# The S5 chain of a two-mixer block, moved ahead of the RWKV inverse

## What is computed

```
h = modulate(rms_norm(x), sh_m, sc_m);  proj = h @ w_in      # 1024 x 2304
z = proj[:, :1792];  u = proj[:, 1792:]                      # z: 14 tiles of 128, u: 4 tiles
z = z + mu * (shift(z) - z)
y_rwkv = group_norm(scan(S = S*w + (S a) b + v k)) + bonus, times a gate
s[t] = abar * s[t-1] + bbar u[t]       # S5: 32 groups of 16 channels, 64 complex states each
y = Re(c s) + d u;  zz = gelu(y);  out = zz * sigmoid(zz @ w_glu + b_glu)
y_s5 = rms_norm(out) * gain
x = x + g_m * (concat(y_rwkv, y_s5) @ w_out)
```

## Time and profile before

| what | us |
|---|---|
| median of 3 executions (1690.25 to 1692.58) | 1690.34 |
| profiled execution, its own time | 1687.02 |
| its span | 1685.2 |
| TensorE busy | 1507.8 |
| VectorE busy | 812.8 |
| ScalarE busy | 581.0 |
| GpSimd busy | 267.4 |

### The profile page before, as it was taken

The page is one execution under the profiler, slowest core; times in us unless marked ns, Lnnn a source line. Parts: engine busy times, 40 slices in busy tenths (PEclk is TensorE's granted clock), DMA queues, the critical chain, the costliest instruction groups (busy, mean ns, idle before and its releaser), DMA issues.

```text
span 1685.2 us, 23778 instructions
## 1 busy us (share of the span) xinstructions
PE 1507.8 (89%) x10024; PEld 1173.4 (70%) x10024; DVE 812.8 (48%) x1291; ACT 581.0 (34%) x1002; POOL 267.4 (16%) x224
## 2 busy tenths in 40 slices
PE   6979877877889999999989899998898999998989
PEld 3657666865668888888866687766686667766767
DVE  7783439623653233223354554546534455445552
ACT  4355231125333222222223434224522444232441
POOL 0000323000101011100012223222201233222220
PEclk9999987988999999999979999998998999999999
DMA  9212572162122222233221121111122111111121
GB/s 367 69 59 61 94 140 104 52 226 88 63 75 88 100 94 94 95 125 100 89 88 40 48 76 63 62 39 50 52 99 96 36 63 59 67 65 36 50 88 63
DMA packets 51849, 144.17 MB, mean 86 GB/s; under 512 B 13216, under 2 KB 17952, under 8 KB 50976
## 3 DMA queue, kind: packets, MB, share of 16 engines
q1 hardware_dynamic: 51744, 142.65, 26.4%
HBM read 137.95 MB, written 4.69 MB: 85 GB/s over the span
## 4 chain that ended last, share of the span: by engine, by line
PE 69%; DVE 14%; ACT 9%; issue 4%; POOL 2%; DMA 1%; SPq 0%; DVEq 0%; ACTq 0%
PE b L391 68%; ACT arena L2103 5%; DVE arena L1245 4%; DVE ring L1245 2%; DVE arena L1253 2%; ACT ring L2106 1%; PE b L394 1%; ACT L2103 1%; POOL arena L2734 1%; DVE arena L1933 1%; DVE X L1245 1%; ACT arena L2106 1%; DVE arena L2066 1%; DMA arena<-scr_yd 1%; DVE arena L1891 1%
## 5 line engine op out<-in xcount | busy, mean ns | idle before, releaser
L391 PE MATMUL b<-tile,ring 128*128 128x512 f32 x2288 | 702.9, 402 | 19.8 <-DVE ring L1245 9.2
L391 PE MATMUL b<-HR,ring 128*128 128x512 f32 (+1 forms) x1888 | 626.2, 408 | 63.1 <-DVE ring L1245 35.1
L391 PEld LDWEIGHTS b<-tile,ring 128*128 128x128 f32 x2288 | 437.5, 192 | 127.6 <-issue 19.5
L391 PEld LDWEIGHTS b<-HR,ring 128*128 128x128 f32 (+1 forms) x1888 | 363.6, 193 | 165.2 <-issue 61.0
L1245 DVE TENSOR_TENSOR ring<-ring,ring 128x1024 fp32r<-128x1024 f32 x186 | 256.1, 1379 | 299.9 <-ACT ring L2106 299.0
L391 PE MATMUL b<-arena 64*64 64x64 f32 (+10 forms) x3072 | 237.5, 289 | 42.9 <-issue 24.6
L2106 ACT ACTIVATE ring<-ring 128x1024 fp32r<-128x1024 f32 x186 | 195.7, 1054 | 213.9 <-PE b L391 213.4
L391 PEld LDWEIGHTS b<-arena 64*64 64x64 f32 (+5 forms) x3072 | 153.6, 150 | 115.8 <-issue 80.7
L2106 ACT ACTIVATE arena<-b 128x512 f32<-128x512 f32 (+3 forms) x136 | 74.4, 570 | 254.3 <-PE b L391 206.3
L1245 DVE TENSOR_TENSOR arena<-arena 128x512 f32<-128x512 f32 (+7 forms) x194 | 100.3, 549 | 71.2 <-ACT arena L2103 50.2
L2731 POOL TENSOR_TENSOR tile<-arena,tile 128x512 fp32r<-128x512 f32 x38 | 51.0, 1348 | 462.2 <-ACT tile L2106 462.2
(11 more groups left out here) (112 smaller groups left out, 1018.8 us busy)
## 6 DMA issues: line engine op xcount, KB each, us to landing
ring<-in_ws SPq DMA_DIRECT2D x218, 512.0 KB, 3.5
arena<-in_ws SPq DMA_DIRECT2D x15, 512.0 KB, 15.4
arena<-in_lw SPq DMA_DIRECT2D x2, 1280.0 KB, 5.6
X<-in_xT SPq DMA_DIRECT2D x2, 1024.0 KB, 6.2
arena<-scr_kpad SPq DMA_DIRECT2D x8, 256.0 KB, 12.5
X<-in_xT SPq DMA_DIRECT2D x1, 2048.0 KB, 15.3
outT<-X SPq DMA_DIRECT2D x8, 256.0 KB, 2.0
arena<-in_cst SPq DMA_DIRECT2D x1, 1088.0 KB, 5.0
```

What stands on the lines that cost most here:

```text
L391: return self.e.matmul(out, lhsT, rhs, start=start, stop=stop, skip_group_check=True)
```

## The change

The strings and the order of the tiles:

```diff
-PREP = "zpzpzpzpzp" + "zmzmpzmpzmpzpzpz"
-MIX = ("s" + "rrr" + "s" + "rrrr" + "a" + "rrrrrr" + "a" + "rs" * 4 + "rrs" * 5 + "a" + "rrs" * 4 + "a" + "rrs" * 6
-       + "rrrrr" + "a" + "rrrrs" + "rrrsr" + "a" + "r" + "s" + "rr" + "a" + "rr" + "s" + "rr" + "a" + "rr" + "a" + "ssss" + "ga"
-       + "s" + "g" + "s" + "oo" + "g" + "oo")
+U_TILES = [14, 15, 16, 17]
+PREP = "zpzzpz" + "smzpm" + "szpmzp" + "ssss" + "zps" + "zpss" + "zpss" + "zps" + "zps"
+MIX = ("rrsrrsrrsrrrsrarrra" + "rrrrrra" + "rrrrsrrsa" + "rrrrrrsa" + "rrrrrrrra" + "rrrsrrrra" + "rrrrrrr" + "rrrrarrrr"
+       + "ras" + "rs" * 6 + "r" + "gogoogo")
```

The four u tiles come first of the twelve that PREP makes; PREP now also plays s1 to s13. VectorE's last table chunks go beside u tiles, two to a tile; its seven last carry steps become two wide ones (`T` and `power` cover all 7x7 elements of 16 groups at once):

```diff
-    def in_proj(self):
+    def in_proj(self, tables):
+        for n in U_TILES:
+            self.blocks(8)
+            for _ in range(2):
+                next(tables, None)
+            yield
+        self.wait_ge(self.k.s("tab"), "end")
...
-        for i in range(7):
-            step(Sv[:, :, :, 1:8, i], Sv[:, :, :, 0:7, 7], power(k.P8R[:, i, :], 7), power(k.P8I[:, i, :], 7),
-                 T[0][:, :, :, 0:7], T[1][:, :, :, 0:7], *(["states"] if i == 6 else []))
-            yield
...
+        for ri, op in ((0, ALU.subtract), (1, ALU.add)):
+            rest = Sv[:, ri, :, 1:8, 0:7]
+            V(T[2 * ri], ends[ri], power(k.P8R), ALU.mult)
+            V(T[2 * ri + 1], ends[1 - ri], power(k.P8I), ALU.mult)
+            self.wait_ge(dve, SOFAR)
+            V(rest, rest, T[2 * ri], ALU.add)
+            self.wait_ge(dve, SOFAR)
+            V(rest, rest, T[2 * ri + 1], op, *(["states"] if ri else []))
+            yield
```

The ks products go to two banks, four groups side by side in four column groups of 32, and two copies of 128x512 take the place of eight of 16x512. Their home moves to z tile 10's place, so tile 10 waits for the write to kpad, which is now four DMAs:

```diff
-        for g4 in range(8):
-            ps = self.take(("ks", g4))
...
+        for b in (0, 1):
+            ps = self.take(("ks", b))
+            for i in range(4):
                 for ri in range(2):
-                    ins = self.mm(o, k.BB[par:par + 64, ri, gp, :],
-                                  k.W[par:par + 64, ri, gp, 0:8, :].rearrange("p d c -> p (d c)"), ri == 0, ri == 1)
+                    for q in range(4):
+                        g = 16 * b + 4 * i + q
+                        f, gp = slice(64 * (g % 2), 64 * (g % 2) + 64), g // 2
+                        at = 256 * ri + 16 * gp
+                        ins = self.mm(ps[32 * q:32 * q + 32, i * 128:i * 128 + 128], k.BBw[f, at:at + 32],
+                                      k.W[f, ri, gp, 0:8, :].rearrange("p d c -> p (d c)"), ri == 0, ri == 1)
...
+        if n == 10:
+            self.wait_ge(k.s("kpad", 16), "k")
```

On Sync the eight TT loads become one step of their own, s17, and wait for the states, whose temporaries lie in TT's place:

```diff
-        for i in range(15):
-            if i < 4:
-                self.wait_ge(k.s("s5_pe"), ("e", 1, 1))
-                for t in (2 * i, 2 * i + 1):
-                    self.e.dma_start(k.TT[16 * t:16 * t + 16, :, :],
...
+        for _ in range(10):
+            yield
+        self.wait_ge(k.s("kpad", 16), "k")
+        self.wait_ge(k.s("s5_dve"), "states")
+        for t in range(8):
+            self.e.dma_start(k.TT[16 * t:16 * t + 16, :, :],
```

More of the change, by code:

```diff
@@ L601, in in_proj @@
         k = self.k
-        for n in Z_ORDER[6:] + [14, 15, 16, 17]:
+        for n in U_TILES + Z_ORDER[6:]:
             ps = self.take(("in", n))
@@ L624, in s5_apply @@
                 yield
-        for _ in range(15):
+        for _ in range(11):
             yield
@@ L1284, in program @@
             self.shifted(n)
-        for _ in tables:
-            pass
-        self.wait_ge(k.s("tab"), SOFAR)
-        self.play(PREP, z=self.in_proj(), p=self.prep())
-        self.play(MIX, r=self.rwkv(), s=self.s5_apply(), a=self.ada_columns(), g=self.group_norm(), o=self.begin_outs())
+        s5 = self.s5_apply()
+        self.play(PREP, z=self.in_proj(tables), p=self.prep(), s=s5)
+        self.play(MIX, r=self.rwkv(), s=s5, a=self.ada_columns(), g=self.group_norm(), o=self.begin_outs())
         x1 = k.s("x1")
@@ L1578, in in_proj @@
             self.shifted(n)
-            yield
-        for n in range(4):
-            self.blocks(8)
             yield
@@ L2251, in s5_matrices @@
         pe, act = k.s("mat_pe"), k.s("mat_act")
-        self.wait_ge(k.s("norm_dve"), ("h1", "x", 7))
-        for g4 in range(8):
-            g0 = 8 * (g4 // 2) + g4 % 2
-            self.wait_ge(pe, ("ks", g4))
-            self.cp(k.KS[:, g0:g0 + 7:2, :],
-                    k.bank["ks", g4][0:16, :].rearrange("p (g d) -> p g d", g=4)).then_inc(*act.inc(("ks", g4)))
-            if g4 % 4 == 3:
-                yield
+        for b in (0, 1):
+            self.wait_ge(pe, ("ks", b))
+            self.cp(k.KS[:, 4 * b:4 * b + 4, :].rearrange("p g d -> p (g d)"), k.bank["ks", b][:, :]).then_inc(*act.inc(("ks", b)))
+        yield
         for g in range(0, 16, 2):
@@ L2279, in in_proj @@
         k = self.k
+        self.wait_ge(k.s("norm_dve"), ("h1", "x", 7))
+        for n in range(4):
+            self.blocks(8)
+            self.wait_ge(k.s("dense"), ("in", 14 + n))
+            self.cp(k.U[:, n], k.bank["in", 14 + n][:, :].rearrange("p (j t) -> p t j", t=8)).then_inc(*k.s("u").inc(n))
+            yield
         for n in Z_ORDER[6:]:
@@ L2282, in in_proj @@
             self.shifted(n)
-            yield
-        for n in range(4):
-            self.blocks(8)
-            self.wait_ge(k.s("dense"), ("in", 14 + n))
-            self.wait_ge(k.s("kpad", 16), "k")
-            self.cp(k.U[:, n], k.bank["in", 14 + n][:, :].rearrange("p (j t) -> p t j", t=8)).then_inc(*k.s("u").inc(n))
             yield
@@ L2747, in program @@
             self.e.memset(k.prep(n)[3][:, :, 0], 1.0).then_inc(*k.s("ones_pool").inc(n))
-        self.play(MIX, r=self.rwkv(), s=self.s5_apply())
+        s5 = self.s5_apply()
+        self.play(PREP, s=s5)
+        self.play(MIX, r=self.rwkv(), s=s5)
         for n in range(DFF_T):
@@ L2756, in s5_apply @@
         k = self.k
-        for _ in range(2 + 4 + 15 + 2 + 2 + 4 + 1):
+        for _ in range(2 + 4 + 11 + 2 + 2 + 1 + 4 + 1):
             yield
@@ L2992, in s5_matrices @@
         yield
-        yield
-        self.wait_ge(k.s("mat_act"), ("ks", 7))
-        self.e.dma_start(d["kpad"].rearrange("g c n -> c g n")[:, :, 112:240], k.KS).then_inc(*k.s("kpad", 16).inc("k"))
+        self.wait_ge(k.s("mat_act"), ("ks", 1))
+        for q in range(4):
+            self.e.dma_start(d["kpad"].rearrange("(i q) c n -> q c i n", q=4)[q, :, :, 112:240],
+                             k.KS[32 * q:32 * q + 16]).then_inc(*k.s("kpad", 16).inc("k"))
         yield
```

54 lines of the change are left out of this document (31 added, 23 removed).

## The result

The changed kernel takes 1705.09 us (median of 19 executions, 1694.09 to 1714.68), the kernel before 1691.83 beside it: ratio 1.0077, 95% interval 1.006 to 1.0095. It is 13 us slower; 1674 was forecast, faster. The profiled execution has a time of 1701.19 us and a span of 1699.4, against 1687.02 and 1685.2. TensorE is busy for 1519.1 us (1507.8 before), VectorE for 801.0 (812.8).

The account below looks back on a forecast made before the run. TensorE was taken to bound the kernel while it has work, with losses in the first 440 us. Terms -1.8 + 27.2 - 8.8 - 32.7 = -16.1 gave 1670.9, and 3.3 for the median made 1674; range 1655 to 1688.

Parts of the forecast that it names:

- PREP: First stage, 102.8 us before: second-tile gap of 7 us goes, VectorE becomes the bound; 1.8 us gained in sum.
- the 7.9 of the rival: ks products in PREP: alternating row halves in one bank take 7.9 us instead of 3.9, total 1678; chance 0.1.
- Grams: Stage before the inverse: carries on VectorE, then queued TT and a2 loads, delay it; 64.5 us for 37.3, +27.2.
- Inverse to scan: Stage from first inverse product to scan's end: waits and gaps leave, glu and norm enter; 161.9 to 153.1, -8.8.
- Clock: Inverse to scan: 11.6 us lost to the clock before, 7 after, plus 2 to recover; -2.6 us.
- Issue gaps: Inverse to scan: 14.2 us of TT-load gaps (9.6 and 4.6) leave, falling where TensorE waits anyway.
- if issue gaps return in the inverse: Sign in the inverse that the forecast is wrong; the other was a2's wait missing.
- the VectorE terms: Inverse to scan: 9.2 us of VectorE waits go, YS's wait grows 1.4, the norm's root adds 4.
- Tail: After the scan: glu, norm and last columns have left, one chain of 25.6 us remains of 58.3; -32.7.
- The slower one: Inverse: instructions arrive late beside yd, u2, YS and x transfers, 15.5 us more gaps; slower 0.1, no change 0.06.
- The a2 loads don't wait: End of grams: inverse starts at about 236 when TensorE is ready, 13 us less, 1661; chance 0.25.
- its rival: Wide carry in the grams no cheaper than narrow: 13.2 us for 15.7, states 4 us later, 1678; chance 0.1.

## Why the prediction was wrong

**PREP: the mechanism right, the time 1.6 us short.** The gap at the second tile is gone, and ks takes 3.7 us, the taken 3.9 and not the 7.9 of the rival. TensorE's row in 105.5 to 110:

```profile
L392 PE MATMUL b<-arena 64*32 64x128 f32 x128 | 3.7, 270 | 0.0
```

The Trainium skill, in "TensorEngine Tiling (Array Packing)", Gotcha 1, says that different row tiles cannot access one PSUM bank at the same time; the trace does not agree, since these 128 products alternate row halves in one bank and run at 0.23 ns a column, the rate of the columns' row. VectorE became the bound as walked: waits of 5.45, 2.70 and 3.25 us for 5.1, 4.8 and 3.6. What the sum hid is its size: the matrix parts alone save 16.0 us (86.80 for 102.80), and e's 4.6 with 11.4 of waits for VectorE give all of it back.

**Grams: right, 2.4 us short.** s14 took 9.6 us for 10.7, the wide steps 6.9 and 4.95 for 7.0 and 4.9, the states stood at 222.4 for 221.3. The delay came as three gaps, 6.92, 6.15 and 2.49 us, and not as one of 9 at r5, and one collision with GpSimd cost s14 3 us where four were to cost 4. The mechanism was in the text; that it was a choice of place and not a price of the change was not: six to eight gram steps later the same carry costs the grams nothing, and the kernel gains 24 us.

**Inverse to scan: the step that failed.** "In sum 161.9 - 4.6 - 9.2 - 14.2 + 16.4 + 1.4 + 4 - 2.6 = 153.1": two terms were mis-sized. *Clock*, "7 after with longer busy stretches, and 2 to recover": TensorE is busy for 143.3 us with the work for which the sum had 130.2 (121.0 of the earlier trace rows less 4.6, plus 16.4, less 2.6), 13.1 more, and the mean granted clock fell where it was to rise. That this is clock and not work can be worked out from the two traces. TensorE's busy time times the missing share of the granted clock, added up over windows of 1 us, is an estimated 16.6 us before and 26.9 after, 10.3 more where the sum had 2.6 less. What is left of the busy time, 104.3 and 116.4 us, grew by 12.1, and the work terms make 11.8 (16.4 less 4.6). The text counted fewer waits and so a better clock. In fact yg moved to a place behind an issue gap, 3.35 us from 267.6. The clock was granted in full again from 254 on, after the gaps of the grams, a2 included; 0.7 us behind this gap it fell to 0.50 and stayed there until 288.6, though TensorE was busy throughout. yg's first 96 matmuls took 14.09 us:

```profile
271.57 14.09 PE L392 MATMUL b<-X,arena 128*128 128x64 f32 x96
```

Behind the inverse they take 7.50; moving yg with yd, YS and glu there is worth 12 to 15 us. *Issue gaps*: 11.2 us left by the sum, 19.5 measured, 8.3 more. The "14.2 us of issue gaps of the TT loads" did leave the stage: 7.24 stand in r13, where TensorE would have waited for a2's weights anyway. What was too small is the rest: beside yd a gap of 3.38, beside YS and x 3.40, beside weights' loads 1.50 and 4.08, all in 64x64 products, and 3.35 ahead of yg. The forecast's own sign, "if issue gaps return in the inverse", came true. 13.1 and 8.3, less 0.5 at the VectorE terms (11.1 for 11.6), are the 20.8 us within 0.1.

The VectorE terms hold a wrong reading that did no harm. "9.2 us of waits for VectorE behind s15 to s20" was taken from 17.7 us in a window that ends at 487, and 2.3 of these lie behind the stage; in the stage 15.4 stand, and 8.1 without YS. YS cost 6.0 us for the 8.6 put, the norm's root 5.1 for 4: both waits were there as described.

**Tail: right, 3.4 us short**: 29.0 for 25.6; a wait of 4.01 us for VectorE's last chain is still ahead of the first full output tile.

**The rivals.** The slower one named one of the two mechanisms. That its 19.5 us for a share of 0.65 is also the measured 19.5 is chance: it meant the gaps of yd, u2, YS and x alone, 15.5 more than the sum had, and the 19.5 measured are all issue gaps of the stage, 8.3 more than the sum had. So its price for the gaps was about twice too high, and it had nothing for the clock, the larger of the two terms. "The a2 loads don't wait" did not come, and where the wait was taken away the inverse's start, 12.6 us earlier, was worth 5. The wide carry saves 5 to 6 us, where 15.7 less 9.2, 6.5, was put; its rival did not come.

What stays open: why some sets of weights' loads beside 64x64 products cost a gap of 3 to 4 us and others 1.5, what of the 2.1 us in the rest belongs to the change, and what yg is worth without yd, YS and glu; no run was made for these.

## What to carry to other kernels

A chain that is moved early is paid by the engine without slack there, so place each of its pieces by the slack of the windows: the same pieces six to eight gram steps later, with yg behind the inverse, turned 13 us slower into 23 faster. Look at what stands ahead of a load in its queue: an ada group's loads ahead of YS went with a wait of 15.6 us and hid what the glu's place was worth. Price a move with the clock in it: the same block takes twice the time (14.09 us for 7.50) where it runs at half the granted clock. Bulk loads beside very short matmuls cost issue gaps that shrank from 8.83 to 3.35 us with an eighth of the bytes, and a gap of 3 us ahead of a block can take the clock for the whole block.
